# Projections behind the mixing layer: the first unit waits tile by tile, and the lower part of a staged tile is made ahead of the sum

## What is computed

```
merged = (sigmoid(g_ssm) * (o_ssm @ w_br_ssm) + sigmoid(g_attn) * (o_attn @ w_br_attn))
h = h + merged @ w_out
h = h + 0.5 * swiglu(rmsnorm(h, norm_ffn2), ffn2_w_in, ffn2_w_out)
```

## Time and profile before

| | us |
|---|---|
| median of 3 executions | 2141.43 |
| lowest and highest | 2140.23, 2143.84 |
| the profiled execution | 2145.38 |
| its span | 2143.1 |
| TensorE busy | 2027.7 (95%) |
| VectorE busy | 995.0 (46%) |
| ScalarE busy | 752.1 (35%) |
| mean granted TensorE clock | 0.983 of full |

### The profile page before, as it was taken

One profiled execution on the slowest core, in us unless ns is written; L12 is line 12 of the kernel. 1 busy time (PEld: TensorE's weight loads), 2 busy tenths in 40 slices (PEclk: granted clock), 3 DMA queues, 4 the chain that ended last, 5 costly groups with the idle time before them and its releaser, 6 DMA issues. The chain is left out here.

```text
span 2143.1 us, 38584 instructions
## 1 busy us (share of the span) xinstructions
PE 2027.7 (95%) x14875; PEld 1968.5 (92%) x14875; DVE 995.0 (46%) x1613; ACT 752.1 (35%) x1320; POOL 406.2 (19%) x497
## 2 busy tenths in 40 slices
PE   6999999986999989999999999999999999999998
PEld 5999999976888988898889889999999999999997
DVE  4433433453772577257735771323444543343344
ACT  4221221234454445444544454333212322122123
POOL 1000000005544254424441543221000000000000
PEclk9999999988999999999999999999999999999999
DMA  5222222222225222521252215223323222222221
GB/s 143 71 91 79 79 79 79 64 103 70 77 65 166 63 67 69 166 63 61 74 166 63 77 57 160 91 72 130 118 96 121 82 79 79 79 78 79 79 64 59
DMA packets 223338, 190.35 MB, mean 89 GB/s; under 512 B 9600, under 2 KB 211408, under 8 KB 221920
## 3 DMA queue, kind: packets, MB, share of 16 engines
q1 hardware_dynamic: 219520, 173.53, 26.6%
q0 software_dynamic: 3136, 14.81, 2.1%
q10 hardware_dynamic: 544, 0.17, 0.0%
HBM read 169.16 MB, written 19.33 MB: 88 GB/s over the span
## 5 line engine op out<-in xcount | busy, mean ns | idle before, releaser
L1582 PE MATMUL ps<-xah,wh 128*128 128x296 f32 x2352 | 528.3, 306 | 38.4 <-POOL wl L751 18.6
L1582 PE MATMUL ps<-xah,wl 128*128 128x296 f32 x2352 | 522.4, 304 | 0.0
L1582 PE MATMUL ps<-xal,wh 128*128 128x296 f32 x2352 | 517.8, 302 | 0.0
L1582 PEld LDWEIGHTS ps<-xah,wh 128*128 128x128 f32 x2352 | 384.0, 191 | 45.7 <-issue 30.1
L1582 PEld LDWEIGHTS ps<-xal,wh 128*128 128x128 f32 x2352 | 386.1, 191 | 0.0
L1582 PEld LDWEIGHTS ps<-xah,wl 128*128 128x128 f32 x2352 | 382.9, 190 | 0.5
L751 POOL TENSOR_TENSOR wl<-raw,wh 128x512 fp32r<-128x512 f32 (+1 forms) x192 | 236.3, 1238 | 454.2 <-ACT wh L849 453.7
L1582 PE MATMUL ps<-xbh,wh 128*128 128x296 f32 x1312 | 287.4, 301 | 6.0 <-DVE xbl L1208 6.0
L1582 PE MATMUL ps<-xbh,wl 128*128 128x296 f32 x1312 | 286.4, 300 | 0.0
L1582 PE MATMUL ps<-xbl,wh 128*128 128x296 f32 x1312 | 286.0, 299 | 0.0
L1202 DVE TENSOR_TENSOR wl<-raw,wh 128x2048 fp32r<-128x2048 f32 x85 | 194.8, 2292 | 113.4 <-ACT wh L841 88.0
(11 more groups left out here) (250 smaller groups left out, 2372.9 us busy)
## 6 DMA issues: line engine op xcount, KB each, us to landing
raw<-in_ffn_w_in_dram SPq DMA_DIRECT2D x88, 512.0 KB, 4.9
raw<-in_w_in_dram SPq DMA_DIRECT2D x80, 512.0 KB, 4.4
raw<-in_ffn_w_out_dram SPq DMA_DIRECT2D x32, 512.0 KB, 4.0
brow<-acs_rows SPq DMA_DIRECT2D x8, 1184.0 KB, 6.1
raw<-in_w_br_ssm_dram SPq DMA_DIRECT2D x16, 512.0 KB, 4.3
raw<-in_ffn_w_out_dram SPq DMA_DIRECT2D x16, 384.0 KB, 3.4
bias<-bias_rows SPq DMA_DIRECT2D x32, 160.0 KB, 4.0
os_spill<-yT SPq DMA_DIRECT2D x8, 592.0 KB, 3.0
```

What stands on the lines that cost most here:

```text
L1582: ins = pe.matmul(bank(b + a, HALF), w[:, slot, k, j * P:(j + 1) * P], x[:, k, a * HALF:(a + 1) * HALF], start=(k == 0 and w is wh and x i ...
```

## The change

TensorE: the wait on all eight tiles ahead of each projection is gone. The loop of two rounds is written out as four duos, and the first unit of each projection gets `tiles_after`, so it waits for tile k in front of its k-th step. All other waits stay.

VectorE: in parts 0 and 1, `x_lower` moves ahead of the wait on `lin_out` and of the sum. In part 2 it stays behind the sum.

```
@@ VectorE, parts 0 to 2
                             m, b = i * 4 + (2 * n + u), 2 * (2 * n + u)
+                            if part < 2:
+                                x_lower(lo, m, G["full"][:, u:u + 1, :], hi)
                             dve.wait_ge(lin_out, st.out.up())
...
                             if part == 2:
                                 dve.wait_ge(dve_free, st.dve(PRIMED))
-                            src = G["h"][:, bass.ds(m, 1), :] if part == 2 else G["full"][:, u:u + 1, :]
-                            x_lower(lo, m, src, hi)
+                                x_lower(lo, m, G["h"][:, bass.ds(m, 1), :], hi)
@@ TensorE, the four projections
                 xr.up(KT)
-                pe.wait_ge(x_ready, xr())
-                with looped(pe, 2, st.all(), [2, 0, 0, 4, 0, 4]) as i:
-                    for n, s in enumerate((1, 0)):
-                        duo_split()
-                        for u in range(2):
-                            pe.wait_ge(dve_free, st.dve(PRIMED - 1))
-                            unit(s, u, xh, xl, KT, 2 * (2 * n + u))
-                            st.dve.up()
+                for n, s in enumerate((1, 0, 1, 0)):
+                    duo_split()
+                    for u in range(2):
+                        pe.wait_ge(dve_free, st.dve(PRIMED - 1))
+                        unit(s, u, xh, xl, KT, 2 * (2 * (n % 2) + u), tiles_after=xr() - KT if n == u == 0 else None)
+                        st.dve.up()
```

## The result

The changed kernel takes 2127.61 us (median of six executions, 2126.23 to 2131.89) beside 2140.84 for the kernel before (six, 2139.78 to 2145.58): ratio 0.9935, 95% interval 0.9925 to 0.9945. A second comparison gave 2129.15 beside 2141.28: 0.9942, 0.9929 to 0.9956. So it is 12 to 14 us faster. The forecast was 2132.0, 9.4 us faster, in the range 2127.5 to 2137. The way was right, and so were the places of the stops. The gain was sized too small by about 3 us: the forecast is a ratio of 0.9956, outside the first interval, and 0.9935 of the median that the forecast started from, 2141.43, is 2127.5, the very edge of the range. The step that failed is the stop inside D.

What follows compares the result with a forecast made beforehand. TensorE, busy 95%, bounds the kernel; only stops and slow clock at four projections, 17.1 us together, could be won. Savings of 4.62 + 2.23 + 3.23 - 0.64 = 9.44 us from median 2141.43 gave 2132.0 us, range 2127.5 to 2137.

Steps and rivals of the forecast that it cites:

- the stop inside D: Ahead of the third unit of the fourth projection: a new TensorE stop of 4.8 us, ended by VectorE's first sum.
- D: Fourth projection: tile-wise start returns 1.00 us, half clock behind the new stop costs 1.64, so 0.64 us is lost.
- A: First projection: starts behind ScalarE's last gates eviction, stop of 1.05 us at full clock; 4.62 of 5.93 us won.
- B and C: Second and third projections: lower part ahead of the sum makes all eight tiles ready; 2.23 and 3.23 us won.
- the second reason given for them: At B and C: waiting tile by tile would alone do nearly the same as moving the lower part.
- Nothing in this chain moves: In D: h load, issued after tile 7, then split and unit 0's sum keep their times; second duo starts at 1648.93.
- its sign: In the changed kernel's trace: a 4.5 to 5 us stop ahead of D's third unit, pairs 0.49 us apart behind it.
- h landed earlier: In D: the spilled h's load ending sooner, so the new stop is missing; named as showing the forecast wrong.
- Written out: TensorE's projection loops as straight code: same matmuls, back edges cost nothing now, so 0 won.
- The clock as a rival: Executions may also pay slow clock at C, or D's new stop may keep the clock; named 2129 us, chance 0.18.
- The sum: Over the four projections: 4.62 + 2.23 + 3.23 - 0.64 = 9.44 us saved, giving 2132.0 us.
- The slower rival: Four additional stretches of TensorE code each cost a 3.15 us issue gap, 12.6 us in all: 2144.6 us; chance 0.05.

Runs made afterwards that it cites:

- the two halves: Two runs against the kernel before: only TensorE's part of the change, ratio 0.9941; only VectorE's part, ratio 0.9976.
- the second trace: Kernel before and changed kernel each traced again without any edit: ratio of the kernel before 1.0001, of the changed kernel 0.9942.

## Why the prediction was right or wrong

**A, forecast 4.62, measured 4.8 by the first traces and 3.7 by the second.** Right in its mechanism: held next by the eviction, a stop of 1.07 us, full clock. The start came 0.21 us behind the eviction instead of 0.35. The 2.75 us of clock in it are not the same in each execution: at stops of 3.00 to 3.02 us other executions paid 2.79, 1.63 and 0.10. So the size was in part luck.

**B and C, forecast 2.23 and 3.23, measured 2.2 and 3.2 by the first traces, 2.2 and 4.7 by the second,** where C paid for the clock before. Right, and the second reason given for them (the tile-wise wait would do nearly the same alone) was shown by the two halves: each alone removes both stops.

**D, forecast -0.64, measured +0.9 by the first traces and -0.3 by the second. This is the step that failed.** The chain was right to the engine: the load of h, the split, the first sum, the third unit. Wrong was "Nothing in this chain moves", and with it the stop of 4.8 us: it measured 3.26, 3.20 and, with TensorE's part alone, 3.26. From the last pair of C to the third unit's start the chain took 1649.93 - 1630.82 = 19.1 us before, of which the forecast kept 18.1; it took 1631.23 - 1614.59 = 16.6. The load landed 9.1 instead of 10.4 us after its issue, since writing the loops out moved a fetch of TensorE's code out of it (1.3 us), and TensorE followed VectorE's sum after 0.14 instead of 0.35 us. The prediction named 4.5 to 5 us as its sign and "h landed earlier" as a sign of being wrong; the latter came in part. The clock behind the stop cost 1.59, 2.79 and 2.76 us where 1.64 was taken, within the bounds; that the first traces show a gain at D is luck with it. Moving D at once was worth 0.6 us of waiting, against a run with D held back. The Trainium skill, page "TensorE: Matmul & The Clock Gate", section "HAM oscillation — how this bites in real kernels", has each burst behind a wait on a transfer begin at half rate. The traces agree in part: in the second one pairs came 0.64 and 0.49 us apart at once, but in the first one the first three intervals were 0.35, 0.28 and 0.27 us, and half rate followed.

**Written out, forecast 0, measured about 1.4 in the kernel before, by its trace and means.** Starts behind a wait come 0.27 us sooner without the loop at B, C and D, and 0.07 at A (part of which the terms above contain). The time around the span is mostly 0.5 us shorter, a term that the sum didn't have at all. The cause of both stays open, and the measured ratio reaches 1.0000.

**The clock as a rival.** The prediction gave 0.18 to executions that pay at C, too, and named 2129. C did pay in the second trace, but A paid less in it, so the places together cost the same 17 us; the rival's mechanism was there, its sum was not.

**The sum.** By the first traces 4.78 + 2.23 + 3.23 + 0.87 = 11.1 in the stretch; by the second 3.66 + 2.23 + 4.73 - 0.25 = 10.4. With 0.5 to 0.7 around the span that is 10.9 to 11.8, beside 12.1 on the means. It falls within the second comparison's interval (9.4 to 15.2 us) and at or under the edge of the first one's (11.8 to 16.1). Of the 2.7 us by which the means exceed the forecast, the two traces of each kernel give 0.9 to D and 0.8 to C's clock, take 0.4 off at A, and some 0.6 lies around the span; the last 0.8 is open.

**The slower rival** (gaps while written-out code arrives) did not appear in any of the kernels with written-out loops. The code's arrival did matter, but through its traffic on the DMA engines, in the opposite direction.

## What to carry to other kernels

When a wait on all parts of an input is turned into waits on each part, walk the first consumers forward to the next thing that isn't moved: here a load queued behind the last part took back most of what D had to gain, and two small edits that freed it (a split ahead of the wait, a bank wait as loose as the banks allow) were worth 4 us again, a third of the change. The split alone gave a ratio as good as both. Where, as here, the consumer takes a part each 0.8 us and the last part is less than 5.7 us late, tile-wise waits alone do it; making the last part earlier as well was of no further use. And cost a stop and the slow clock behind it apart: the stop repeats to 0.02 us in the kernel before and to 0.06 in the changed one, the clock's share doesn't, so one profile can't size it.

## What the hardware showed that was not expected

- The clock behind a stop: after the stops of 2.96 to 3.02 us ahead of A and C, in four traces, it cost 0.1 us three times, 1.6 twice and 2.7 to 2.8 twice; with the loops written out, after 2.95 and 2.69 us, 0.1 each; behind the longer stops in D (3.04 to 3.97 us, eleven of them) always 1.6 to 2.8; behind those of 1.96 us and less never more than 0.1. TensorE was then at 1.2 instead of 2.4 GHz, pairs 0.49 us apart instead of 0.27. Over these 20 stops of 2.69 us and more there are three prices, 0.1, 1.6 and 2.8, and none between.
- The half clock need not begin at the stop: behind five of D's eleven stops the first two to four intervals between pairs were still at or near full pace (0.27 to 0.38 us).
- A single 16 KB fetch of TensorE's instructions made a 2368 KB load 0.4 to 1.4 us longer, depending on where in the load it fell. Removing a loop moved it, and so did instructions that do nothing, 1100 us earlier.
- A semaphore increment of its own on TensorE took about 0.147 us: 84, 100 and 130 in a row filled 12.3, 14.8 and 19.1 us of a stop that was 10.5 to 10.9 us long without them.
